# An expert layer's end: sums of scattered rows on VectorE, three one-hot experts, result reads begun beside the last weights

## The reference, cut to what matters

```python
out = jnp.zeros_like(ht)
for e in range(N_EXPERTS):
    hid = jax.nn.silu(ht @ e_gate[e]) * (ht @ e_up[e])
    out = out + combine[:, e:e + 1] * (hid @ e_down[e])
...
x = x + gt2 * _hier_moe(h2, router_group, router_expert, expert_w_gate, expert_w_up, expert_w_down)
...
return _rmsnorm(x, final_norm_g), ...
```

## Time and profile before

| what | value |
|---|---|
| median of 3 runs | 1558.73 us (1556.69 to 1560.74) |
| the profiled execution's own time | 1561.74 us |
| its span | 1560.0 us |
| busy: TensorE, VectorE, ScalarE, GpSimd | 1366.2, 598.3, 452.2, 239.4 us |
| bytes moved by DMA | 322.78 MB |
| mean granted TensorE clock | 0.945 of full speed |

### The profile page before, as it was taken

The page is one execution under the profiler, slowest core; times in us unless marked ns, Lnnn a source line. Parts: engine busy times, 40 slices in busy tenths (PEclk is TensorE's granted clock), DMA queues, the critical chain, the costliest instruction groups (busy, mean ns, idle before and its releaser), DMA issues. The chain is left out here.

```text
span 1560.0 us, 30399 instructions
## 1 busy us (share of the span) xinstructions
PE 1366.2 (88%) x13439; PEld 1005.8 (64%) x13439; DVE 598.3 (38%) x1045; ACT 452.2 (29%) x724; POOL 239.4 (15%) x248
## 2 busy tenths in 40 slices
PE   4999999999999996888878999979987888788875
PEld 1788998888998996777767998763333333233322
DVE  3222234452225445555635567542221222112116
ACT  3333243344554543333334543211000000000002
POOL 3000100000112113233400202001111111111116
PEclk9999999999999997999989999969999999999988
DMA  9466442222432120000032264089999999999995
GB/s 335 159 203 206 146 157 68 68 83 89 141 103 68 55 55 23 5 4 4 7 127 68 83 214 155 34 347 403 424 428 426 428 426 427 426 428 426 426 403 197
DMA packets 128554, 322.78 MB, mean 207 GB/s; under 512 B 13849, under 2 KB 99059, under 8 KB 112514
## 3 DMA queue, kind: packets, MB, share of 16 engines
q1 hardware_dynamic: 114224, 289.27, 48.6%
q10 hardware_dynamic: 7522, 15.57, 2.9%
q0 software_dynamic: 6672, 15.95, 2.8%
HBM read 303.25 MB, written 25.11 MB: 210 GB/s over the span
## 5 line engine op out<-in xcount | busy, mean ns | idle before, releaser
L798 PE MATMUL bank<-upper_r 128*128 128x272 f32 x3168 | 419.7, 291 | 5.4 <-DVE upper_r L1037 5.4
L798 PEld LDWEIGHTS bank<-upper_r 128*128 128x128 f32 x3168 | 403.0, 189 | 30.1 <-issue 29.1
L2657 PE MATMUL bank<-upper7b,lower 128*64 128x512 f32 x912 | 254.9, 656 | 74.4 <-issue 73.6
L2657 PEld LDWEIGHTS bank<-upper7b,lower 128*64 128x64 f32 x912 | 84.3, 151 | 208.3 <-issue 206.7
L1014 DVE TENSOR_TENSOR upper_r<-upper,upper_r 128x1024 fp32r<-128x1024 f32 x66 | 82.8, 1255 | 292.5 <-ACT upper_r L571 292.3
L2464 ACT ACTIVATE lower<-bank 128x256 f32<-128x256 f32 x32 | 12.3, 384 | 438.2 <-PE bank L2666 438.2
L3011 DVE COPY lower<-bank 128x512 f32<-128x512 f32 x32 | 22.1, 692 | 278.4 <-PE bank L2657 278.4
L2520 PE MATMUL bank<-upper_r 128*128 128x272 f32 x768 | 103.0, 294 | 2.7 <-DVE upper_r L2906 2.7
L2520 PEld LDWEIGHTS bank<-upper_r 128*128 128x128 f32 x768 | 99.4, 191 | 5.4 <-DVE upper_r L2738 3.1
L2679 PE MATMUL bank<-upper7b,lower 128*64 128x512 f32 x432 | 98.4, 596 | 0.0
L2269 POOL DMA_INDIRECT expert_out<-lower x30 | 44.5, 1484 | 220.8 <-DVE lower L3034 217.2
(11 more groups left out here) (399 smaller groups left out, 1824.0 us busy)
## 6 DMA issues: line engine op xcount, KB each, us to landing
upper7b<-in_expert_w_gate SPq DMA_DIRECT2D x29, 2048.0 KB, 31.3
upper7b<-in_expert_w_up SPq DMA_DIRECT2D x28, 2048.0 KB, 32.9
upper7b<-in_expert_w_down SPq DMA_DIRECT2D x27, 2048.0 KB, 27.9
upper<-in_w_in SPq DMA_DIRECT2D x66, 512.0 KB, 3.8
lower<-in_w_ada SPq DMA_DIRECT2D x23, 1024.0 KB, 5.0
lower<-in_expert_w_down SPq DMA_DIRECT2D x5, 2048.0 KB, 30.0
lower<-in_expert_w_up SPq DMA_DIRECT2D x4, 2048.0 KB, 36.7
lower<-in_expert_w_gate SPq DMA_DIRECT2D x3, 2048.0 KB, 30.7
```

What stands on the lines that cost most here:

```text
L798: m = mm(psum[s][:, c, 0:HALF], w_part[s][:, k, :], h_part[:, k, c * HALF:(c + 1) * HALF], start=k == 0 and w_part is w_high and h_part is ...
L2657: m = nc.tensor.matmul(psum[s][64 * b:64 * b + 64, 1, :], x_t[(e // 2) % 2][:, k, s * BLK:(s + 1) * BLK], w[:, k, :], start=k == 0, stop=k ...
```

## The change

- `E_LAST` is 29: three experts (29, 30, 31) are added through one-hot matrices instead of two, and one scatter falls away. The third matrix is built at expert 10.
- SyncE reads the results of tiles 2 to 4, and `final_norm_g`, as soon as the scatters up to expert 28 have landed. Tiles 0 and 1 are read by GpSimd's own DMA queue, also after those scatters.
- Gate and up of expert 31 are loaded in two halves each; both first halves stand ahead of both second halves. TensorE multiplies the first half, then adds expert 29 into tiles 0 and 1, then waits for the second half.
- All sums of the two places, the residual of tile 4 and the final products of tiles 0 and 1 are done by VectorE; GpSimd computes nothing after its last scatter. VectorE sums tile 0 ahead of `down_scaled` of expert 30 and tile 1 ahead of `down_scaled` of expert 31.
- The PSUM banks are dealt anew, so that the banks of tiles 0 and 1 are free before the last expert is through.

The diff, cut: what is left out renames banks in the expert loop to the three new functions, and drops or renames semaphores.

```diff
@@ -1839,7 +1839,7 @@
-        E_LAST = NE - 2
+        E_LAST = NE - 3
...
-        last_t.append(after_gt1.take(T))
-        last_oh = Region(summing_at, summing_at + 1200).take(5, P)
+        last_t += [after_gt1.take(T) for _ in range(2)]
+        summing = Region(summing_at, summing_at + 1200)
+        last_oh = summing.take(5, P)
...
+        def gu_bank(s):
+
+            return psum[2 * s][:, 1 - s, :]
+
+        def hid_bank(s):
+
+            return psum[1 + s][:, 1, :]
+
+        def dn_bank(s):
+
+            return psum[3][:, s, :]
+
         def y_of(e):
 
-            return x_blk[:, 512 * (e % 2):512 * (e % 2) + 512] if e >= E_LAST else y_blk[e % 2]
+            return x_blk[:, 512 * (e % 2):512 * (e % 2) + 512] if e - E_LAST in (0, 1) else y_blk[e % 2]
...
-            sp.dma_start(weights_of(kind, e), source[e]).then_inc(landed[e % 3], 16)
-
+            if kind == "down" or e < NE - 1:
+                sp.dma_start(weights_of(kind, e), source[e]).then_inc(landed[e % 3], 16)
+            else:
+                sp.dma_start(weights_of(kind, e)[:, 0:4], source[e][:, 0:4]).then_inc(landed[e % 3], 16)
+
+        def load_last_half(sp):
+            for kind, source in (("gate", egate), ("up", eup)):
+                sp.dma_start(weights_of(kind, NE - 1)[:, 4:8], source[NE - 1][:, 4:8]).then_inc(wg_rest_in, 16)
...
-        LAST_AT = {2: 0, 6: 1}
+        LAST_AT = {2: 0, 6: 1, 10: 2}
...
+        def read_results(queue, j, n):
+
+            queue.dma_start(gath[j][0:n].rearrange("t k d -> t (k d)"), ys_v[j * P:j * P + n]).then_inc(gathered[j], 16)
...
@@ -2174,23 +2195,18 @@
                         load_unit(sp, n)
+                        if STREAM[n] == ("up", NE - 1):
+                            load_last_half(sp)
                     sp.wait_ge(gu_mm, r * NE + (NE - 1))
-                    sp.sem_inc(held, 1)
-                    sp.wait_ge(dn_mm, r * NE + (NE - 2))
                     sp.sem_inc(held, 1)
                     for s in range(2):
                         sp.wait_ge(y_out9[s], r * (16 * Y_USES[s]) + 16 * Y_USES[s])
                         sp.sem_inc(held, 1)
+                    for j, n in TILES[2:]:
+                        read_results(sp, j, n)
+                    sp.dma_start(fin_g, I["final_norm_g"].partition_broadcast(P)).then_inc(last_rows_in, 16)
                     for j, n in TILES:
-                        sp.dma_start(gath[j][0:n].rearrange("t k d -> t (k d)"), ys_v[j * P:j * P + n]
-                                     ).then_inc(gathered[j], 16)
-                    sp.dma_start(fin_g, I["final_norm_g"].partition_broadcast(P)).then_inc(last_rows_in, 16)
-                    for j in (2, 0, 3, 1, 4):
...
+                        sp.wait_ge(f_done, r * 5 + (j + 1))
...
@@ -2287,21 +2303,13 @@
                         scatter(r, e)
-                    for j, n in TILES:
-                        g = gath[j]
-                        pool.wait_ge(gathered[j], r * 16 + 16)
+                    for s in range(2):
+                        pool.wait_ge(y_out9[s], r * (16 * Y_USES[s]) + 16 * Y_USES[s])
                         pool.sem_inc(held, 1)
-                        pool.tensor_tensor(g[0:n, 0, :], g[0:n, 0, :], g[0:n, 1, :], ALU.add).then_inc(g_sum, 1)
-                    pool.wait_ge(g_sum, r * 6 + 5)
+                    pool.wait_ge(dn_mm, r * NE + (NE - 3))
                     pool.sem_inc(held, 1)
-                    pool.tensor_tensor(x2[0:DEC, 4, :], x2[0:DEC, 4, :], gath[4][0:DEC, 0, :], ALU.add
-                                       ).then_inc(g_sum, 1)
...
-                    for i, j in enumerate(BY_POOL):
-                        pool.wait_ge(f_scaled, r * len(BY_POOL) + (i + 1))
-                        pool.sem_inc(held, 1)
-                        pool.tensor_tensor(x_fin[j], x2s[i], fin_g, ALU.mult).then_inc(f_pool, 1)
+                    for j, n in TILES[0:2]:
+                        read_results(pool, j, n)
...
@@ -2474,10 +2482,6 @@
-                        if j - 1 in BY_POOL:
-                            act.wait_ge(f_done, r * 8 + NORM_AT[j - 1][0])
-                            nc.scalar.activation(x2s[j - 1], x2[:, j - 1, :], ACT.Copy, scale=sums2[:, j - 1:j]
-                                                 ).then_inc(f_scaled, 1)
...
@@ -2653,8 +2657,13 @@
                     for k in range(KD):
+                        if e == NE - 1 and k == 4:
+                            for j in range(2):
+                                last_down(r, j, 0)
+                            pe.wait_ge(wg_rest_in, r * 32 + 32)
+                            pe.sem_inc(held, 1)
                         for b, w in enumerate(gate_and_up):
...
@@ -2691,6 +2700,8 @@
                     pe.wait_ge(y_done, r * NE + (E_LAST + i + 1))
+                    if j == 1 and i == 0:
+                        pe.wait_ge(hid_done, r * NE + (NE - 1))
...
                         if e == NE - 1:
-                            last_down(r, 0, 0)
+                            for j in range(2):
+                                last_down(r, j, 1)
                         down(r, e)
...
-                    last_down(r, 0, 1)
-                    for j in range(1, 5):
+                    for j in range(2):
+                        last_down(r, j, 2)
+                    for j in range(2, 5):
                         for i in range(NL):
                             last_down(r, j, i)
...
                 def summed(r, j):
-                    v.wait_ge(g_sum, r * 6 + (j + 1))
-                    ve.tensor_tensor(x2[:, j, :], x2[:, j, :], gath[j][:, 0, :], ALU.add).then_inc(x2_sum, 1)
+                    n = TILES[j][1]
+                    g = gath[j]
+                    v.wait_ge(gathered[j], r * 16 + 16)
+                    ve.tensor_tensor(g[0:n, 0, :], g[0:n, 0, :], g[0:n, 1, :], ALU.add).then_inc(g_sum, 1)
+                    v.wait_ge(g_sum, r * 5 + (j + 1))
+                    ve.tensor_tensor(x2[0:n, j, :], x2[0:n, j, :], g[0:n, 0, :], ALU.add).then_inc(x2_sum, 1)
...
@@ -3097,23 +3110,25 @@
-                        if e == NE - 1:
-                            summed(r, 0)
                         if e + 1 < NE:
                             gate_up_copied(r, e + 1)
                         if e % 2 == 0 and e + 2 < NE:
                             rows_copied(r, e // 2 + 1)
+                        if e == NE - 2:
+                            summed(r, 0)
+                        if e == NE - 1:
+                            summed(r, 1)
                         down_scaled(r, e)
-                    summed(r, 1)
                     last_added(r, 0)
                     last_added(r, 1)
                     summed(r, 2)
+                    v.wait_ge(last_rows_in, r * 16 + 80)
                     normed(r, 0)
                     last_added(r, 2)
                     summed(r, 3)
                     normed(r, 1)
                     last_added(r, 3)
-                    v.wait_ge(last_rows_in, r * 16 + 80)
+                    summed(r, 4)
                     normed(r, 2)
                     last_added(r, 4)
                     normed(r, 3)
```

More of the change, by code:

```diff
@@ L1967, in load_unit @@
             source, landed = {"gate": (egate, wg_in), "up": (eup, wg_in), "down": (edown, wd_in)}[kind]
-            sp.dma_start(weights_of(kind, e), source[e]).then_inc(landed[e % 3], 16)
+            if kind == "down" or e < NE - 1:
[5 more added lines that the diff above has]
+                sp.dma_start(weights_of(kind, NE - 1)[:, 4:8], source[NE - 1][:, 4:8]).then_inc(wg_rest_in, 16)
+        wg_rest_in = sem("wg_rest_in")
         yr_free = sem("yr_free")
@@ L2095, in build @@
         f_std = sem("f_std")
+        f_rs = sem("f_rs")
         f_done = sem("f_done")
-        f_scaled = sem("f_scaled")
-        f_pool = sem("f_pool")
         y_final = sem("y_final")
@@ L2107, in build @@
         ys_v = ys_dram.rearrange("(t k b) c -> t (k b c)", k=2, b=2)
-        BY_POOL = (0, 1)
-        x2s = [gath[0][:, i, :] for i in range(2)]
-        NORM_AT = {0: (1, 0), 1: (2, 0), 2: (3, 4), 3: (5, 6), 4: (7, 8)}
+        def read_results(queue, j, n):
+            queue.dma_start(gath[j][0:n].rearrange("t k d -> t (k d)"), ys_v[j * P:j * P + n]).then_inc(gathered[j], 16)
         def first(r):
@@ L2463, in a_round @@
                         act.wait_ge(gu_tr, r * NE + (e + 1))
-                        nc.scalar.activation(act_g, psum[2 + s][:, 0, :].rearrange("p (f t) -> p f t", f=4)[:, :, 0:BLK],
+                        nc.scalar.activation(act_g, hid_bank(s).rearrange("p (f t) -> p f t", f=4)[:, :, 0:BLK],
                                              ACT.Silu).then_inc(silu_done, 1)
@@ L2655, in gate_up @@
                     for k in range(KD):
+                        if e == NE - 1 and k == 4:
[3 more added lines that the diff above has]
+                            pe.sem_inc(held, 1)
                         for b, w in enumerate(gate_and_up):
```

(21 more changed lines are left out.)

7 lines of the change are left out of this document (removed).

## The result

The changed kernel has a median of 1563.44 us (1556.57 to 1568.31, 20 runs), the kernel before 1558.99 us (1555.23 to 1563.15, 20 runs). The ratio is 1.0027, 95% interval 1.0016 to 1.0037: 4.2 us slower, where 2.3 were forecast. That is less than the 0.3% which the forecast took as the bound of "same", but twenty runs a side tell it from no change.

The account below looks back on a forecast made before the run. Weights set the pace until they are in, then VectorE's last stage; -0.8 (S earlier) + 1.3 + 1.75 (last stage) = +2.3 us on the median 1558.73 gives 1561.0 us, range 1556 to 1566.

Parts of the forecast that it names:

- Weights bound until they are in: Expert layer: weight loads set the pace; earlier changes matter only if they take more than TensorE's idle time.
- the third matrix and the PSUM banks free: Building the third one-hot matrix at expert 10 and dealing the PSUM banks anew: cost 0 each.
- Reads earlier, down 30 and 31 later: Result reads 12 us earlier; down 30 lands at 1524.8, down 31 at 1531.5, up 31 stays at 1517.1.
- Halves: 4.0 us gained, 0.9 left: Gate/up 31 in halves ends at 1522.0 instead of 1525.97; waiting for down 30 leaves 0.9 of the 4.0 us.
- down 30 "ends (3.65)": TensorE after gate/up 31: down 30 starts at 1524.8, takes 3.65 us and ends at 1528.45.
- rival B: Reads come in bulk ahead of down 30, or its wait lowers TensorE's clock (1.7 us): 1563.0; chance 0.17.
- Forecast (A): Main case for the whole kernel: +2.3 us, median 1561.0, down 31 starting when its weights land; chance 0.45.
- S 0.8 earlier: S, the end of scaling expert 31's result on VectorE, comes at 1535.9 instead of 1536.66.
- Last stage 3.05 dearer: VectorE after expert 31's scaling: stands 1.3 us, then needs 21.0 against 19.25 us, 1.3 + 1.75 dearer.
- GpSimd's company at 4.95 us: VectorE's 19.25 us after expert 31's scaling: 14.3 clean, the other 4.95 us caused by GpSimd working beside it.
- C: Tile 1 lands late and VectorE stands before expert 31's scaling; slower by over 0.3%, at worst 1567.2; chance 0.13.
- D: Reads fit the DMA's idle share: down 30 at 1522.4, expert 31 scaled at 1533.0, 1558.1, no change; chance 0.18.

Follow-up runs that it names:

- one-queue kernel: Changed kernel with the results of tiles 0 and 1 also read by SyncE's queue, behind down 31, and summed one place later on VectorE; ratio to before 0.9993.
- the kernel in which TensorE adds: Changed kernel with the two places of tiles 2 and 3 added by TensorE into PSUM instead of by VectorE; ratio to before 1.0025.
- filler of four: Changed kernel with four extra TensorE products, result overwritten, between gate/up 31 and down 30; ratio to before 1.0008.
- the two GpSimd runs: Changed kernel and one-queue kernel, each with the first adds of tiles 2 to 4 on GpSimd; ratios to before 1.0015 and 0.9997.
- the first of its two kernels: One-queue kernel with tiles 3 and 4 summed by accumulating DMAs, 0.9958 to before; the second also moves expert 30's one-hot products after down 31, 0.9958.

## Why the prediction was right in sign and range, and short in size

- *Weights bound until they are in; the third matrix and the PSUM banks free.* Nothing in the runs speaks against it: the one-queue kernel has both and is level with before. They were not taken out by themselves.
- *Reads earlier, down 30 and 31 later.* Forecast t = 22.9 and 29.6 (1524.8 and 1531.5), measured 23.9 and 30.6; up 31 was in at t = 16.6, as TensorE came back for it, where 15.2 was forecast: the reads delayed it too. In the six kernels with two queues whose landings I have, down 30 lands at 22.7 to 25.0 and up 31 at 15.3 to 17.5, so 1.0 us is within what one execution differs from another. That the two queues take turns is borne out by the landings: down 30 came 3.4 of the possible 4.9 us late, and tile 1 (t = 28.8) ahead of down 31 and ahead of SyncE's tiles. The Trainium skill (DMA: Bandwidth & Descriptors, Issuing engines are not separate DMA queues) has it so, and the trace agrees: with both queues at work (1514 to 1520) the windows give 397 to 430 GB/s, with one 427. The second queue brought no bandwidth, it only chose who waits.
- *Halves: 4.0 us gained, 0.9 left.* The gain was 3.7 (gate and up 31 end at t = 20.3, forecast 20.1). **What failed is the next term: down 30 "ends (3.65)".** I saw the wait of 2.8 us in front of it and put the clock's fall into rival B at 1.7 us, because no row showed a fall after less than 4.05 us of idle time. The wait was 3.71, the clock fell, and it cost 3.0 (in the kernel in which TensorE adds, 1.7). Forecast (A) had down 31 bound by its weights; it was bound by TensorE's chain, 2.8 us after they had landed. The filler of four shows the forecast's mechanism: down 31 starts at its landing (t = 30.6), S is at 35.0 and the tail 60.6. The forecast had S at 34.0 and a tail of 60.4, so that its tail is met there by two errors of opposite sign, S too early and the last stage too long. What a wait of 2.8 us does to the clock stays untested: no tail shows a wait of TensorE between 1.81 and 3.70 us.
- *S 0.8 earlier.* It is 3.1 later: 3.0 of clock, 1.0 of landing, less 0.1 net of smaller terms.
- *Last stage 3.05 dearer.* The list of lengths was right (1.22, 1.28, 0.15, the stand of 1.3), the sum too large by 0.9. The 0.5 us for hand-overs was my guess, and its sign was wrong: a dependent instruction starts some 0.03 us after the one ahead, one without a dependence some 0.1 us before it has ended (1536.19 + 2.35 = 1538.54, next start 1538.46), which gives back 0.35 over the list. It cost 2.1.
- *GpSimd's company at 4.95 us.* It left out the same overlap: row by row, five instructions of VectorE after S were 5.65 us longer in the kernel before than clean (2.76, 2.05, 1.87, 2.06 and 3.17 us). As a price for giving work back it does not carry over, as the two GpSimd runs show.
- *Rivals.* B was the case, by its second half. That its 1563.0 is so near the measured 1563.44 is partly luck: it has the clock at 1.7 and the last stage 0.9 too long, and S at t = 36.0 where 37.9 was measured. Its first half, reads in a bulk ahead of down 30 (t = 25.4), is neither shown nor refuted: the changed kernel has 23.9, the one in which TensorE adds 25.0. C did not happen: tile 1 was summed before down 31 had ended. D's times are what the one queue makes: S at 31.2, D had 31.1.

The forecast had seen the step that failed, but only inside rival B, at a chance of 0.17. The measured 4.2 us and the tail's 5.2 agree within the spread of single executions; which part of that 1.0 is chance stays open.

## What to carry to other kernels

When a transfer is moved ahead, write down which weight lands later by it, and what the engine that waits for that weight does in the meantime: a wait moved from one product to the next gained nothing here, and it took TensorE's clock along. Judge a change at the end of a program from a point shortly before it, since the spans of single executions hid 5 us here. Before work is handed to another engine, look up what the first engine does in just those microseconds; DMA that accumulates was the only helper here whose work did not lengthen another engine's instructions; it cost one wait of 1.0 us in the first of its two kernels and none in the second.

## What the runs showed of the hardware that was not expected

- TensorE's clock fell to 1.2 of 2.4 GHz around every wait of 3.7 us or more that these tails show (3.70, twice 3.71, 4.05, 4.07, 4.69 us). Behind five of them the next products took 5.35 to 6.63 us instead of 3.65, behind the one of 4.05 us 8.78 instead of 7.09, and the two waits of 3.71 us cost 1.7 and 3.0 us. The clock stayed at 1.00 after the 1.81 us of the earlier trace rows, and when filler products stood in the wait for down 30.
- A product of 512 float32 columns over the whole array takes 0.9 us (3.70 for four); pairs on half arrays take the same 0.9 us for both (7.09 us for the eight pairs of gate and up).
- A float32 sum by two accumulating DMAs of 512 KB each, one after the other, took a median of 7.4 us apiece to land, beside the other reads.
